# Hybrid encoder on one Trainium2 core: a mirrored table of turns, imaginary halves summed by TensorE, and the last state-space tiles reordered

## The reference, cut to what matters

```
h = h + even_mixer(rmsnorm(h), ...)            # ends with  concat @ w_out
h = h + conv_ffn(rmsnorm(h), ...)
u = rmsnorm(h)
# S5, in chunks:  x_t = lam_bar * x_{t-1} + b_bar u_t  (complex),  y = real(c @ x)
y = y + d * u;  y = gelu(y)
y = y * sigmoid(y @ w_glu + b_glu);  h = h + y
h = h + conv_ffn(rmsnorm(h), ...)
out = rmsnorm(h)
```

## Time and profile before

| | |
|---|---|
| median of 3 runs | 2249.06 us (2248.68 to 2249.78) |
| profiled execution | 2247.46 us |
| its span | 2245.7 us |
| granted clock, mean | 0.965 |
| busy: PE, DVE, ACT, POOL | 2090.8, 1622.6, 977.7, 637.9 us |

### The profile page before, as it was taken

How to read it: one execution, slowest core, us unless ns; L and a number is a source line. 1 busy time by engine, 2 the same in 40 slices (tenths; PEclk the granted TensorE clock), 3 DMA queues, 4 the chain that set the end, 5 groups by cost and what they waited for, 6 DMA issues and landing times.

```text
span 2245.7 us, 39772 instructions
## 1 busy us (share of the span) xinstructions
PE 2090.8 (93%) x12768; PEld 1789.0 (80%) x12768; DVE 1622.6 (72%) x2329; ACT 977.7 (44%) x1386; POOL 637.9 (28%) x729
## 2 busy tenths in 40 slices
PE   5999998994999999998999966979999999999997
PEld 4878876783888888887888865868888888888886
DVE  6686544775788888887777765778888888875555
ACT  4344343332444444443545522544444444444442
POOL 8962100694000000004888765520000000002221
PEclk8999999797999999999999988989999999999998
DMA  3545433352755555554777785535555555556664
GB/s 129 171 159 180 151 120 113 110 184 65 251 186 184 183 182 186 187 187 157 234 221 233 231 264 161 187 127 181 185 184 184 185 186 186 187 189 190 185 182 133
DMA packets 146676, 398.71 MB, mean 178 GB/s; under 512 B 22704, under 2 KB 47920, under 8 KB 146624
## 3 DMA queue, kind: packets, MB, share of 16 engines
q1 hardware_dynamic: 129056, 381.26, 53.7%
q10 hardware_dynamic: 17568, 16.78, 2.3%
HBM read 377.02 MB, written 18.87 MB: 176 GB/s over the span
## 4 chain that ended last, share of the span: by engine, by line
PE 62%; DVE 18%; issue 8%; POOL 7%; DVEq 2%; ACT 2%; ACTq 1%; DMA 1%; POOLq 0%; SPq 0%
PE bank L316 33%; PE bank L315 17%; DVE lo L296 6%; DVE cgv L1125 3%; PE bank L312 2%; DVE cgv L1122 2%; DVE sumt L330 2%; PE bank L1505 1%; PE bank L1507 1%; PE bank L1506 1%; POOL ut L770 1%; DVE ut L366 1%; DVE th L1282 1%; PE bank L313 1%; ACT lowt L325 1%
## 5 line engine op out<-in xcount | busy, mean ns | idle before, releaser
L316 PE MATMUL bank<-xx,hi 128*128 128x512 f32 x3510 | 1255.9, 400 | 0.0
L315 PE MATMUL bank<-xx,lo 128*128 128x256 f32 x3510 | 989.6, 282 | 0.0
L296 DVE TENSOR_TENSOR lo<-raw,hi 128x1024 fp32r<-128x1024 f32 x698 | 885.0, 1299 | 132.8 <-ACT hi L289 124.3
L289 ACT ACTIVATE hi<-raw 128x1024 fp32r<-128x1024 f32 x698 | 710.2, 1052 | 338.9 <-PE bank L316 264.3
L316 PEld LDWEIGHTS bank<-xx,hi 128*128 128x128 f32 x3510 | 664.4, 189 | 152.6
L315 PEld LDWEIGHTS bank<-xx,lo 128*128 128x128 f32 x3510 | 668.1, 190 | 9.8
L316 PE MATMUL bank<-aa,hi 128*128 128x512 f32 x1344 | 474.3, 394 | 0.0
L315 PE MATMUL bank<-aa,lo 128*128 128x256 f32 x1344 | 376.7, 280 | 2.3 <-DVE lo L296 2.3
L316 PEld LDWEIGHTS bank<-aa,hi 128*128 128x128 f32 x1344 | 253.0, 188 | 59.2
L315 PEld LDWEIGHTS bank<-aa,lo 128*128 128x128 f32 x1344 | 253.0, 188 | 4.8 <-DVE lo L296 3.3
L1125 DVE SCALAR_TENSOR_TENSOR cgv<-sumt,par,cgv 128x255 f32<-128x255 f32 x368 | 180.5, 491 | 54.4 <-DVE cgv L1125 26.1
(11 more groups left out here) (302 smaller groups left out, 1893.9 us busy)
## 6 DMA issues: line engine op xcount, KB each, us to landing
raw<-in_up SPq DMA_DIRECT2D x344, 512.0 KB, 3.9
raw<-in_down SPq DMA_DIRECT2D x160, 448.0 KB, 4.1
raw<-in_w_in SPq DMA_DIRECT2D x98, 512.0 KB, 4.1
raw<-in_w_out SPq DMA_DIRECT2D x32, 512.0 KB, 3.3
raw<-in_down SPq DMA_DIRECT2D x32, 512.0 KB, 3.5
raw<-in_glu SPq DMA_DIRECT2D x32, 512.0 KB, 3.6
s_c<-cp ACTq DMA_DIRECT2D x16, 256.0 KB, 4.8
s_p<-ut ACTq DMA_DIRECT2D x32, 128.0 KB, 5.1
```

Source lines behind the costliest of these rows:

```text
L289: A.activation(hi[:, s, :], raw[:, s, :], ACT.Copy).then_inc(hi_done, 1)
L296: V.tensor_tensor(lo[:, s, :], raw[:, s, :], hi[:, s, :].bitcast(f32), SUB).then_inc(lo_done, 1)
L315: TE.matmul(bank[:, L:], lo[:, s, w], x2[:, k, 0, :], start=False, stop=False)
L316: last = TE.matmul(bank[:, :], hi[:, s, w], x2[:, k, :, :], start=False, stop=k == total - 1)
```

## The change

It has three parts.

**The table.** Column 32 (`MID`) now holds the turn by zero instead of column 0. The doublings up to 32 columns are the same instructions, written 32 columns further on. The doubling from 32 to 64 columns, 4 quarters of 6 instructions, is gone. In its place POOL writes column 0 with two instructions (the cosine and the negated sine of the 32-fold turn) after tile 3, and ACT copies columns 63 to 33 in reverse into columns 1 to 31, once for the cosine and once with sign -1 for the sine, 128 partitions x 64 x 31 elements each. ACT does so behind its last weight split of `w_out` and ahead of the root of the norm.

**The imaginary half.** POOL writes the two products straight into `xo`, which now has a full 4-part buffer for each of two tiles, and subtracts in place for the real half. The addition is gone: PE multiplies both imaginary products with the same weights, so each tile's state term has 24 matmuls where it had 16. POOL's multiplications for tile k now wait for the outputs of tile k-2 themselves; before, only the sums did.

**The order at the end.** `by_sin` of even and odd tiles swap banks 0 and 1, so bank 1 is free for the first GLU tile after the scan of tile 14. The first 8 blocks (of 128 weight rows) of the first GLU tile go ahead of the outputs of tile 14 (before: ahead of those of tile 15), and 4 more of it and 6 of the second tile go ahead of the outputs of tile 15. On ACT the rounding of y's third part and two weight splits go ahead of the last Gelu.

```diff
-                c, s = rot_c[:, pr, 0:n], rot_s[:, pr, 0:n]
+                c, s = rot_c[:, pr, MID:MID + n], rot_s[:, pr, MID:MID + n]
...
                 if i == 3:
                     next_unit()
-                if i in (3, 5, 7):
-                    x = (i - 3) // 2
-                    chain(turns(32, x * PAIRS // 4, (x + 1) * PAIRS // 4))
-            turns(32, 3 * PAIRS // 4, PAIRS).then_inc(rot_new, 1)
+                    G.tensor_scalar(rot_c[:, :, 0], rho[:, 0, 0, :], 1.0, None, MUL)
+                    G.tensor_scalar(rot_s[:, :, 0], rho[:, 0, 1, :], -1.0, None, MUL).then_inc(rot_new, 1)
...
                 g.wait_ge(q_new, kt + 1)
                 if kt >= 2:
-                    g.wait_ge(xo_new, kt - 1)
+                    g.wait_ge(y_done, kt - 1)
                 for a in range(2):
-                    ins = G.tensor_tensor(w[:, a, :, :, 1:], qq[:, o, :, :, 0:C5 - 1],
+                    ins = G.tensor_tensor(xo[o][:, 2 * a:2 * a + 2, :, 1:], qq[:, o, :, :, 0:C5 - 1],
                                           rot[:, s, a, :, 0:C5 - 1].unsqueeze(1).broadcast_to([P, 2, 4, C5 - 1]), MUL)
                 chain(ins)
-                if kt >= 2:
-                    g.wait_ge(y_done, kt - 1)
-                G.tensor_tensor(xo[:, o, 0, :, 1:], w[:, 0, 0, :, 1:], w[:, 1, 1, :, 1:], SUB)
-                G.tensor_tensor(xo[:, o, 1, :, 1:], w[:, 0, 1, :, 1:], w[:, 1, 0, :, 1:], ADD).then_inc(xo_new, 1)
+                G.tensor_tensor(xo[o][:, 0, :, 1:], xo[o][:, 0, :, 1:], xo[o][:, 3, :, 1:], SUB).then_inc(xo_new, 1)
...
+            a.wait_ge(rot_new, 1)
+            for x, sign in ((rot_c, 1.0), (rot_s, -1.0)):
+                ins = A.activation(x[:, :, 1:MID], x[:, :, C5 - 1:MID:-1], ACT.Copy, scale=sign)
+            ins.then_inc(rot_whole, 1)
...
-            gelu_high(2)
-            act_split(a, B_GLU + LEAD, 8, 0, range(0, 2))
+                if kt == 15:
+                    gelu_high(2)
+                    act_split(a, B_GLU + LEAD, 8, 0, range(0, 2))
             gelu_high(3)
...
-                    for part in range(2):
+                    for x, part in ((0, 0), (1, 1), (2, 1)):
                         for r in halves:
-                            last = TE.matmul(bank[r, cols[m]], c_op[r, s, 4 * part + m, :], xo[r, o, part, m, :],
-                                             start=False, stop=part == 1, skip_group_check=True)
+                            last = TE.matmul(bank[r, cols[m]], c_op[r, s, 4 * part + m, :], xo[o][r, x, m, :],
+                                             start=False, stop=x == 2, skip_group_check=True)
...
-            for kt in range(3, KT + 2):
+            for kt in range(3, KT + 1):
...
+            p.wait_ge(q_new, KT - 1)
+            glu_part(0, 0, 8).then_inc(block_used, 1)
+            chunk_outputs(KT - 2)
+            glu_part(0, 8, 12)
             p.wait_ge(q_new, KT)
-            glu_part(0, 0, 8).then_inc(block_used, 1)
+            glu_part(1, 0, 6)
             chunk_outputs(KT - 1)
-            glu_part(0, 8, 12)
-            glu_part(1, 0, 12)
+            glu_part(1, 6, 12)
             glu_part(0, 12, KT).then_inc(block_used, 1)
```

More of the change, by code:

```diff
@@ L28 @@
 C5 = L // T5
+MID = C5 // 2
 SLOTS = 4
@@ L208, in hybrid_encoder @@
         ych = uu
-        turned_back = [x.rearrange("p a b -> p (a b)").rearrange("p (a z m c) -> p a z m c", a=2, z=2, m=4)
-                       for x in (ut[:, 0, :, :], tab[:, 1:3, :])]
-        xo = ut[:, 1, :, :].rearrange("p a b -> p (a b)").rearrange("p (s z m c) -> p s z m c", s=2, z=2, m=4)
+        xo = [ut[:, 1, :, :].rearrange("p a b -> p (a b)").rearrange("p (z m c) -> p z m c", z=4, m=4),
+              tab[:, 1:3, :].rearrange("p a b -> p (a b)").rearrange("p (z m c) -> p z m c", z=4, m=4)]
         by_cos = (cgv[:, :, :].rearrange("p a (m c) -> p a m c", m=4),
                   tab[:, 0, :].rearrange("p (a m c) -> p a m c", a=2, m=4))
-        by_sin = [acc[o][:, :].rearrange("p (a m c) -> p a m c", a=2, m=4) for o in range(2)]
+        by_sin = [acc[1 - o][:, :].rearrange("p (a m c) -> p a m c", a=2, m=4) for o in range(2)]
         rdat = lowt[:, :, :].rearrange("p s (m c) -> p s m c", m=4)
@@ L252, in hybrid_encoder @@
         s5_dma_c = [sem("s5_dma_c0"), sem("s5_dma_c1")]
-        rot_new, rot_out = sem("rot_new"), sem("rot_out")
+        rot_new, rot_whole, rot_out = sem("rot_new"), sem("rot_whole"), sem("rot_out")
         z_done, neg2_new, ln_done, lf_new = sem("z_done"), sem("neg2_new"), sem("ln_done"), sem("lf_new")
@@ L660, in turns @@
                 chain(G.tensor_tensor(w[:, 3], s, gr, MUL))
-                G.tensor_tensor(rot_c[:, pr, n:2 * n], w[:, 0], w[:, 1], SUB)
-                return G.tensor_tensor(rot_s[:, pr, n:2 * n], w[:, 2], w[:, 3], ADD)
+                G.tensor_tensor(rot_c[:, pr, MID + n:MID + 2 * n], w[:, 0], w[:, 1], SUB)
+                return G.tensor_tensor(rot_s[:, pr, MID + n:MID + 2 * n], w[:, 2], w[:, 3], ADD)
             def next_unit():
@@ L673, in _ @@
             g.wait_ge(mix_new, KT)
-            G.memset(rot_c[:, :, 0], 1.0)
-            G.memset(rot_s[:, :, 0], 0.0)
+            G.memset(rot_c[:, :, MID], 1.0)
+            G.memset(rot_s[:, :, MID], 0.0)
             for part, x in enumerate((rot_c, rot_s)):
-                G.tensor_scalar(x[:, :, 1], rho[:, 1, part, :], 1.0, None, MUL)
+                G.tensor_scalar(x[:, :, MID + 1], rho[:, 1, part, :], 1.0, None, MUL)
                 ins = G.tensor_scalar(rho[:, 0, part, :], rho[:, 1, part, :], 1.0, None, MUL)
@@ L761, in _ @@
             g.wait_ge(s5_dma_p, 32 * KT)
-            chain(G.memset(xo.rearrange("p s z m c -> p (s z m) c")[:, :, 0], 0.0))
+            for x in xo:
+                chain(G.memset(x.rearrange("p z m c -> p (z m) c")[:, 0:3 * 4, 0], 0.0))
             for kt in range(KT):
                 s, o = kt % SLOTS, kt % 2
-                w = turned_back[o]
                 g.wait_ge(q_new, kt + 1)
                 if kt >= 2:
-                    g.wait_ge(xo_new, kt - 1)
+                    g.wait_ge(y_done, kt - 1)
                 for a in range(2):
-                    ins = G.tensor_tensor(w[:, a, :, :, 1:], qq[:, o, :, :, 0:C5 - 1],
+                    ins = G.tensor_tensor(xo[o][:, 2 * a:2 * a + 2, :, 1:], qq[:, o, :, :, 0:C5 - 1],
                                           rot[:, s, a, :, 0:C5 - 1].unsqueeze(1).broadcast_to([P, 2, 4, C5 - 1]), MUL)
                 chain(ins)
-                if kt >= 2:
-                    g.wait_ge(y_done, kt - 1)
-                G.tensor_tensor(xo[:, o, 0, :, 1:], w[:, 0, 0, :, 1:], w[:, 1, 1, :, 1:], SUB)
-                G.tensor_tensor(xo[:, o, 1, :, 1:], w[:, 0, 1, :, 1:], w[:, 1, 0, :, 1:], ADD).then_inc(xo_new, 1)
+                G.tensor_tensor(xo[o][:, 0, :, 1:], xo[o][:, 0, :, 1:], xo[o][:, 3, :, 1:], SUB).then_inc(xo_new, 1)
             pool_squares(g, chain, 4, 0, glu_new)
@@ L898, in ffn @@
                         up_pair(i, False)
-                    a.wait_ge(rot_new, 1)
+                    a.wait_ge(rot_whole, 1)
                     for part, x in enumerate((rot_c, rot_s)):
```

## The result

The changed kernel takes 2223.33 us (median of 4 runs, 2221.14 to 2226.34) where the kernel before took 2248.87 beside it on the same chip (2246.19 to 2249.78): a ratio of 0.9888, with an interval of 0.9876 to 0.9901. That is 25.5 us less. The forecast was 2224. The profiled execution took 2224.03, with a span of 2222.3 (before: 2247.46 and 2245.7) and a granted clock of 0.968 (before 0.965).

What follows compares the result with a forecast made beforehand. PE's wait for POOL's backlog behind `w_out`, POOL and close-by loads in S5, and a tail stall were taken as the bound. Gains 18.1 + 4.0 + 2.0 = 24.1 us off 2247.46 gave 2223.4, stated as 2224; range 2216 to 2232.

Steps and rivals of the forecast that it cites:

- The backlog: Norm behind `w_out`: without the doublings POOL has caught up by tile 15, so PE starts its sum 16.6 us earlier.
- halfway price of 2.37: Norm behind `w_out`: us per POOL square-and-sum pair, between 1.49 with DVE quiet and 3.24 beside DVE's work.
- The lower end of 14.8: Norm behind `w_out`: gain in us if every POOL pair beside DVE's splits cost 3.24 under an exclusive port lock.
- The freed scalings: After the norm's sum: DVE's 8 scalings no longer run beside POOL's fourth-quarter doubling, 2.2 us gained.
- The copies: ACT's two table copies ahead of the norm's root: 2.33 us each, cost 0 with 3.6 us of cover.
- The 0.7 for a slow start: First up-projection: PE starts at 1.2 GHz after its wait, so 0.7 us taken off, bounds 0 and 1.5.
- first half: S5 stage to tile 9's wait: tile 4's outputs, from which SP's load list runs, come 2.5 us earlier.
- The second half: S5 stage after that: tiles 8 to 11 bring 0, tiles 12 to 14 bring 2.1 us less 0.6 for loads.
- the loads decide all of S5: S5 stage: loads set the pace, 2 us or less of the 4.0 stay, 2229 us; chance 0.13.
- The free wait for y of tile k-2: S5 stage: POOL's new wait ahead of its multiplications costs nothing, as PE needs 1.7 of POOL's 3.3 us.
- The slower case: S5 stage and GLU: PE at 1.2 GHz becomes the bound, 2255 us, slower than before; chance 0.03.
- Part 3, forecast 2.0: Tail, last scan to first complete GLU tiles: 21.9 us in place of 23.9, 2.0 gained, bounds 0 and 3.

Runs made afterwards that it cites:

- the quarter put back: Changed kernel with one quarter's table doubling put back on POOL behind tile 3's square of `w_out`, results unused: 2227.7 us.
- the kernel with six copies: Changed kernel with ACT's two mirror copies of the table made three times over: 2226.02 us.
- rot6: Changed kernel with 6 slots for `rot` in place of 4, loaded two tiles further ahead: 2215.42 us.
- the imaginary half alone: Kernel before with only POOL's addition removed and 24 matmuls in place of 16 per tile's state term: 2244.2 us.
- one quarter late: Changed kernel with one quarter's table doubling put back on POOL behind tile 15's square of `w_out`, results unused: 2224.02 us.
- ACT's order alone: Kernel before with only ACT's rounding of y's third part and two weight splits ahead of the last Gelu: 2243.6 us.

## Why the prediction was right, and where it was off

**What bounds the kernel.** Right. PE's 19.10 us and the S5 stage were where time was to be had, and the reason given for the first, POOL's arrears, was tested by the quarter put back.

**Part 1, forecast 18.8 before the clock, measured 19.2.** The backlog: PE's wait fell by 16.45 (forecast 16.6). POOL's pairs took (498.82 - 478.30) / 9 = 2.28 us each, near the halfway price of 2.37. The lower end of 14.8, worked out from every pair at 3.24, did not come. The Trainium skill, "SBUF — State Buffer", section "Who interferes with whom", was weighed there. Its exclusive lock stands with the trace as to the form: the square takes either 0.61 or 1.46 to 1.54. What failed as an estimate was to let every instruction meet it: of the 18 squares and sums in those nine pairs, 8 took the longer time. The freed scalings: 2.2 forecast, 5.47 - 3.26 = 2.21 measured. The copies: 2.33 each forecast, 1.85 measured, cost nothing with 4.4 us of cover, and beyond the cover they do cost, as the kernel with six copies shows. The 0.7 for a slow start lies within the scatter of the next piece and is not confirmed.

**Part 2, forecast 4.0, measured 1.4 in this trace: the mis-sized term.** Its first half, "Those come 5 x 0.7 = 3.5 us earlier, less 0.5 for the longer group, less 0.5", gave 2.5 before tile 9's wait; the trace gives 0.2. The outputs of tile 4, from which SP's list runs, came no earlier (`t_op` for tile 8 is issued 22.9 behind POOL's first turn in both), for two reasons. I had let POOL's saving run through tiles 0 to 4, but DVE already waited for `rot` of tile 5 before (0.93). Before, that load was issued as soon as POOL was done with tile 1. In the changed kernel POOL is done 1.4 earlier, but SP's list stands for something else: the load of `t_op` for tile 4 is ahead in it and waits for PE's outputs of tile 0, whose longer group takes 2.83 in place of 1.97:

```profile
1301.21 2.83 PE L1698 MATMUL bank<-ut,c_op 64*64 64x64 f32 x48 [4.93 <-POOL ut L771]
1303.62 0.72 POOL L771 TENSOR_TENSOR tab<-tab 128x252 f32<-128x252 f32 x1
1304.12 0.38 SPq L471 DMA_DIRECT2D t_op<-s_t  x1
```

So the load of `rot` is issued 8.6 behind POOL's first turn, hardly before the 8.8 of the kernel before, and it takes 1311.21 - 1305.56 = 5.65 us until DVE goes on. POOL came to tile 4 only 0.7 earlier (16.8 against 17.5). And PE's longer group took 2.48 in place of 1.15 there, 1.3 more and not 0.5, at a granted clock of 0.71 in the window around it:

```profile
1316.00:1320.00 4.00, 2.92 (x65) 2.81 (x62) 3.75 (x9) 0.90 (x2) 3.84 (x5) 0.71 0.86 240
```

That ate the rest. The second half, forecast 1.5, measured 25.16 - 23.95 = 1.2 from the start of tile 8 to the last scan. DVE's wait before tile 13 stayed (2.33 before, 2.41 now), and it is `rot` here too, though the row names PE, whose input states of that tile were done by 1347.1:

```profile
1345.95 0.59 SPq L463 DMA_DIRECT2D rot<-s_rot  x1
1345.96 1.11 PE L1678 MATMUL bank<-uu,p_op 64*64 64x64 f32 x32
...
1350.28 0.69 DVE L1380 TENSOR_TENSOR tab<-bank,rot 128x512 f32<-128x512 f32 x1 [2.41 <-PE bank L1678]
```

The rival "the loads decide all of S5" (2 us or less through) is what this trace shows, and `rot6` confirms its mechanism. But one trace is not enough for the size. Five of the kernels have S5 as it is after the change or the imaginary half alone: their S5 pieces are 62.61, 61.70, 61.43, 59.69 and 59.68, 61.0 in the mean. Five have it as before: 63.45 to 64.31, 63.8 in the mean. So Part 2 is worth 2.8 us, with 1.4 in the changed kernel's own trace and 4.1 in the best. In the two shortest (six copies, one quarter late) tile 4's group took 1.61 and POOL started tile 8 at 36.4, 2.5 earlier than before: there the forecast's first half came as worked out. The mechanism stands, and what I had sized too small is what PE's longer group and the list behind it take back in some executions. Why PE's group is short in some and long in others was not tried. The medians give 4.7 for Part 2 alone, with 2 us of interval either way, which agrees with 2.8.

**The free wait for y of tile k-2.** Nearly right: it shows once in POOL's column, 0.82 us long:

```profile
1346.28 3.29 POOL L768 TENSOR_TENSOR tab<-qq,rot 128x504 f32<-128x504 f32 x2 [0.82 <-PE bank L1698]
```

It comes where PE ran at the lower level. The two levels of PE's group of 48:

```profile
1339.05 2.83 PE L1698 MATMUL bank<-ut,c_op 64*64 64x64 f32 x48 [4.55 <-POOL ut L771]
...
1356.27 1.61 PE L1698 MATMUL bank<-ut,c_op 64*64 64x64 f32 x48 [2.75 <-POOL ut L771]
```

The first is at 1.2 GHz (granted 0.50 from 1339 to 1343), the second at 2.4 GHz (granted 1.00 from 1355 to 1359), although PE had waited before both. The slower case stayed away because it needed 14 of 16 tiles at the lower level: here the groups of tiles 0, 4 and 8 took 2.48 to 2.83 us and that of tile 9 took 1.94. A stage in which all of them are slow was never seen, and so its price was not tested.

**Part 3, forecast 2.0, measured 3.5.** Up to the low half of the last part the steps hold: tile 15's outputs forecast 12.8 behind the scan, Gelu at 1372.49 - 1359.54 = 12.95; its low half forecast at 18.7, PE goes on with it at 19.1. Then I charged six blocks (2.2) and 1.0 for slow blocks and hand-overs; the first tile needed only its last two, 1.29 us. The same mix-up stands in my reading of the rows: at 1401.20 only the first tile was complete, after 20 blocks and not 24, so that they took 0.44 us each in the mean and not 0.37. The stall that was to go went, and the last move of y is late next, as said. Which part of the edit does it I did not say; ACT's does it alone. With ACT's order alone PE runs through its blocks without a stop, and with both it is done sooner and stands 3.16 for y, so the two come out alike (20.20 and 20.23).

**The sum.** 24.1 us were forecast between the two profiled runs and 23.4 came. Part of that closeness is luck: Part 1 came 0.4 over, Part 3 1.5 over and Part 2 2.6 short, while the four other pieces add up to -0.7, which is by chance what I had put down for the clock.

## What to carry to other kernels

When PE waits for an engine with little total work, look whether that engine ever idled before the wait: if not, everything it does ahead of that point is on the path, minus the slack it had, and it can be moved to an engine with a wait of its own in its column, up to the length of that wait. In a ring of engines fed by a fixed list of loads, making one engine faster brings only what the load with the longest lead time lets through: measure the start of the decisive load against the ring's start, and if it doesn't move, add slots rather than shorten instructions. An edit of order is best split by engine before one pays for all of it.

## What was not expected

PE sometimes stops in the middle of a group of matmuls with nothing named as the releaser:

```profile
1327.79 1.26 PE L1698 MATMUL bank<-ut,c_op 64*64 64x64 f32 x20 [2.00 <-issue]
```

The other 28 of this group had started at 1324.76. In the trace before there is one of 1.54 (1350.66), in `rot6` one of 3.16 (1331.39), both with 22 of a group's 32 records still to come. Here it falls into a time in which DVE waits for `rot` anyway; in `rot6` it holds DVE up, and stops of 2 to 3 us are as large as the scatter of the S5 piece.

No run varied them, but the traces say where they come from. Eleven of the 13 have such stops within a group of this stage, 25 of over 0.4 us, the longest 3.88 in the imaginary half alone. All 25 stand in the same place modulo 256 (to one) when the instructions on PE's side, weight loads and waits included, are counted from the start of the trace. And each ends 1.3 to 1.6 us after a transfer of 16 KB has ended on the DMA queue that the page calls `q8 instruction`. So what PE waits for is its next block of instructions. The stage is also where many loads of operands are under way at once; whether these delay the blocks was not tested. The imaginary half adds 256 matmul records and as many weight loads, two such blocks, to the stage (31 transfers on that queue in the whole trace, 29 before): a price of it that neither the prediction nor its sum has.

Loads of the same 256 KB differ much in length: the 12 of `rot` within the changed kernel's S5 stage took 2.6 to 6.8 us from issue to landing. The one issued at 1326.69 let DVE go on at 1333.05, 6.4 us later, and over the 16 us from 1318 on, into which the two blocks of GLU weights fall, the three loads of `rot` have a median of 6.3.
